# Retention samples in row and column groups, gated transposes moved into the chunk loop, on-chip memory reordered

## What is computed

```python
def retention_step(s, (qc, kc, vc)):          # per head, state s is 128 x 128
    att = einsum("bihd,bjhd->bhij", qc, kc) * decay
    o = einsum("bhij,bjhe->bihe", att, vc) + einsum("bihd,bhde->bihe", qc * q_dec, s)
    s = s * c_dec + einsum("bjhd,bjhe->bhde", kc * k_dec, vc)

def gla_step(s, (qc, kc, vc, gc)):            # per head, state s is 128 x 256
    o = einsum("bhij,bjhe->bihe", att, vc) + einsum("bihd,bhde->bihe", qc * exp(b), s)
    s = s * exp(b_last) + einsum("bjhd,bjhe->bhde", kc * exp(b_last - b), vc)
```

## Time and profile before

| | us |
|---|---|
| runs shown | 2237.97, 2239.32, 2248.58 |
| median | 2239.32 |
| profiled execution, its own time | 2247.53 |
| its span | 2245.7 |
| PE busy | 2123.9 (95%) |
| DVE, ACT, POOL busy | 997.2, 762.3, 197.0 |
| stretch of the retention samples on PE | 153.25 to 172.19 |
| gated steps of heads 2 and 3 on PE | 1367.29 to 1413.43 |
| first half of `out1` with the gated samples | 1414.76 to 1473.15 |

### The profile page before, as it was taken

How to read it: one execution, slowest core, us unless ns; L and a number is a source line. 1 busy time by engine, 2 the same in 40 slices (tenths; PEclk the granted TensorE clock), 3 DMA queues, 4 the chain that set the end, 5 groups by cost and what they waited for, 6 DMA issues and landing times.

```text
span 2245.7 us, 30502 instructions
## 1 busy us (share of the span) xinstructions
PE 2123.9 (95%) x12346; PEld 1865.4 (83%) x12346; DVE 997.2 (44%) x1671; ACT 762.3 (34%) x1314; POOL 197.0 (9%) x454
## 2 busy tenths in 40 slices
PE   7999869999889999999999999899979999999997
PEld 6889649898668999999988888679857899999996
DVE  5451463334434444444343457552542544444443
ACT  3311442234423432322323446233542433233232
POOL 2020111000110000000000124110010000000001
PEclk9999888999999999999999999999999999999999
DMA  6232313124552212222222121432373122222221
GB/s 195 68 120 90 130 56 94 57 85 141 209 189 75 76 57 76 76 85 75 76 88 60 55 75 43 147 140 94 141 282 115 58 75 76 76 85 76 75 76 51
DMA packets 111048, 219.94 MB, mean 98 GB/s; under 512 B 6994, under 2 KB 52350, under 8 KB 110844
## 3 DMA queue, kind: packets, MB, share of 16 engines
q1 hardware_dynamic: 89920, 143.80, 19.3%
q0 software_dynamic: 20416, 72.09, 9.0%
q10 hardware_dynamic: 576, 2.10, 0.2%
HBM read 201.03 MB, written 18.24 MB: 98 GB/s over the span
## 4 chain that ended last, share of the span: by engine, by line
PE 88%; DVE 5%; ACT 3%; DMA 3%; issue 1%; POOL 0%; SPq 0%; ACTq 0%; DVEq 0%; POOLq 0%
PE bank L738 14%; PE bank L740 14%; PE bank L739 14%; PE bank L800 7%; PE bank L802 7%; PE bank L798 7%; PE bank L797 5%; PE bank L801 4%; PE bank L799 4%; PE bank L1092 1%; PE bank L761 1%; PE bank L1003 1%; PE bank L1070 1%; PE bank L1119 1%; DMA vcX<-cache_mem_v 1%
## 5 line engine op out<-in xcount | busy, mean ns | idle before, releaser
L1869 DVE TENSOR_TENSOR w_lo<-raw,w_hi 128x1024 fp32r<-128x1024 f32 x265 | 319.7, 1222 | 604.3 <-ACT w_hi L1395 600.4
L1395 ACT ACTIVATE w_hi<-raw 128x1024 fp32r<-128x1024 f32 x265 | 274.2, 1052 | 327.1 <-PE bank L740 266.8
L738 PE MATMUL bank<-w_hi,hT_lo 128*128 128x512 f32 x720 | 290.5, 403 | 7.5 <-DVE Sb L2377 4.0
L800 PE MATMUL bank<-hT_lo,w_hi 128*128 128x384 f32 (+1 forms) x856 | 289.3, 338 | 0.0
L798 PE MATMUL bank<-hT_hi,w_lo 128*128 128x384 f32 (+1 forms) x856 | 289.3, 338 | 0.0
L802 PE MATMUL bank<-hT_hi,w_hi 128*128 128x384 f32 (+1 forms) x856 | 289.3, 338 | 0.0
L740 PE MATMUL bank<-w_hi,hT_hi 128*128 128x512 f32 x720 | 285.8, 397 | 0.0
L739 PE MATMUL bank<-w_lo,hT_hi 128*128 128x512 f32 x720 | 285.7, 397 | 0.0
L797 PE MATMUL bank<-hT_hi,w_lo 128*128 128x256 f32 (+1 forms) x856 | 239.6, 280 | 0.0
L799 PE MATMUL bank<-hT_lo,w_hi 128*128 128x256 f32 (+1 forms) x856 | 239.0, 279 | 0.0
L801 PE MATMUL bank<-hT_hi,w_hi 128*128 128x256 f32 (+1 forms) x856 | 239.0, 279 | 0.0
(11 more groups left out here) (362 smaller groups left out, 3160.6 us busy)
## 6 DMA issues: line engine op xcount, KB each, us to landing
raw<-w_ffn_gate SPq DMA_DIRECT2D x44, 512.0 KB, 4.0
raw<-w_ffn_up SPq DMA_DIRECT2D x44, 512.0 KB, 5.1
raw<-w_ffn_down SPq DMA_DIRECT2D x22, 1024.0 KB, 5.0
kcX<-cache_mem_k POOLq DMA_DIRECT2D x16, 1024.0 KB, 7.6
vcX<-cache_mem_v POOLq DMA_DIRECT2D x16, 1024.0 KB, 7.3
raw<-w_in_even SPq DMA_DIRECT2D x14, 1024.0 KB, 5.2
raw<-w_in_odd SPq DMA_DIRECT2D x12, 1024.0 KB, 5.1
raw<-w_cq SPq DMA_DIRECT2D x8, 1024.0 KB, 7.8
```

The costliest lines, as they stand in the source:

```text
L738: pe.matmul(out, wl, xh, start=first, stop=False)
L800: pe.matmul(ob, wh, hT_lo[:, k, HA:TOK], start=False, stop=False)
L1395: act.activation(w_hi[:, g % W_SLOTS, 0:n], raw[:, q % 2, UNIT * i:UNIT * i + n], ACT.Copy).then_inc(*hi_made.mark(c, u))
L1869: dve.tensor_tensor(w_lo[:, s, 0:n], raw[:, q % 2, UNIT * i:UNIT * i + n], flat(w_hi[:, s, 0:n]), ALU.subtract).then_inc(*lo_made.mark(c, u))
```

## The change

**Memory.** `w_hi`, `w_lo` and `hT` now come first, then the shared region `U`, then `raw`, `x` and the rest. The four retention states get other places: head 0 over `kd0`'s first tiles, heads 1 and 2 over `xn`, head 3 over `gain`. SP's load of the cross-attention gain waits for the store of the last retention state instead of the bias row. ACT waits for that store before the key projection's evacuation and no longer before the query projection's.

**Retention samples.** POOL issues the loads of heads 1 to 3 right after the first norm and the bias rows, that of head 0 after prompt tile 1, and clears the (smaller) `qz0` then. `ret_padded` makes all padding at once, before the last prompt tile's mask. PE reads in column groups: the query tile has 192 columns per head, and four sequences sit in four 32-column groups. It adds in row groups: two masks split even and odd sequences, four groups of 32 rows go to four banks. Reads of all heads come first, then the additions of heads 0 and 1, one column tile of the next projection, the additions of heads 2 and 3. DVE's state updates are sixteen of 256 columns instead of eight of 512.

**Gated transposes.** `MIXED_IN` puts the transposes of the first six half-tiles into the steps of heads 2 and 3, with ACT's copies and DVE's subtractions; the transposes of (1, 3), the split of unit 0 and the last state update move too.

```diff
-MIXED_FIRST = [(0, 0), (0, 1), (0, 2), (0, 3), (1, 0), (1, 1)]
+MIXED_IN = {(1, t): [(0, t)] + [(1, t - 2)] * (t >= 2) for t in range(TP)}
...
-        Sb0 = [at(f"Sb0{h}", off, [P, NB, P]) for h, off in enumerate((0, 20480, 4096, 24576))]
-        qz0 = at("qz0", 10240, [P, 2, 1152])
-        kz0 = [at("kz0a", 55296, [P, NB, P]), at("kz0b", 30720, [P, NB, P])]
+        Sb0 = [over(f"Sb0{h}", a, [P, NB, P]) for h, a in enumerate((U + 20480, xn_at, xn_at + 4096, gain_at))]
+        qz0 = at("qz0", 10240, [P, H, 192])
+        kz0 = at("kz0", 55296, [P, 2, 512])
...
+            pool.wait_ge(*aux_full.at("nT", "mix0", T - 1, 1))
+            for h in range(1, H):
+                ret_state(h)
             for t in range(TP - 1):
                 head_rstd(("ret", t), t, H, P)
                 if t == 1:
                     ret_state(0)
-                    ret_state(1)
-            pool.wait_ge(*aux_full.at("att0", TP))
-            pool.memset(qz0[:, :, :], 0.0).then_inc(*pool_done.mark("qz0"))
+                    pool.memset(qz0[:, :, :], 0.0).then_inc(*pool_done.mark("qz0"))
...
-                for b in range(NB):
-                    ins = pe.matmul(o[:, P * h:P * h + P], qz0[:, h % 2, P * b:P * b + P], Sb0[h][:, b, :], start=False, stop=b == NB - 1)
+                for c in range(2):
+                    for g in range(4):
+                        ins = pe.matmul(o[32 * g:32 * g + 32, e], qz0[:, h, 48 * g + 16 * c:48 * g + 16 * c + 32], Sb0[h][:, 2 * g + c, :],
+                                        start=False, stop=c == 1, tile_position=(0, 32 * g))
...
+            def add_pair(hp):
+                banks = [(aux if g < 2 else lin).open(pe, "s0s", hp, g) for g in range(4)]
...
             for i in range(4):
+                if i < 2:
+                    add_pair(i)
                 cols_tile(("in0", 0), "mix0", P * i, i, last=i == 3)
...
                     proj_tile(c, "mix1", tt)
+                for m in MIXED_IN.get((hp, t), ()):
+                    mixed_turn(*m)
                 pe.wait_ge(*dve_done.at("qe", hp, t))
...
-            for q, t in MIXED_FIRST:
-                mixed_turn(q, t)
+            mixed_turn(1, 2)
             out1(0)
-            mixed_turn(1, 2)
             out1(1)
             read_state(0)
             read_state(1)
+            mixed_turn(1, 3)
             add_state(0)
-            mixed_turn(1, 3)
             out1(2)
             read_state(2)
             read_state(3)
             add_state(1)
             out1(3)
-            add_state(2)
             for hp in range(2):
                 mixed_turn(hp, TP)
             pe_done.after("mixed", 1)
+            add_state(2)
+            out1(TP)
             add_state(3)
-            out1(TP)
```

More of the change, by code:

```diff
@@ L445, in gains @@
                 if nm == "cross0":
-                    sp.wait_ge(*put["bias"].at("row"))
+                    sp.wait_ge(*put["st0"].at(H - 1))
                 if nm == "cross1":
@@ new lines, in _ @@
+            ins.then_inc(*aux_full.mark("o0", TP))
+            def add_pair(hp):
+                banks = [(aux if g < 2 else lin).open(pe, "s0s", hp, g) for g in range(4)]
+                for hh in range(2):
+                    for c in range(2):
+                        for g in range(4):
+                            r = slice(32 * g, 32 * g + 32)
+                            e = slice(P * (2 * hp + hh), P * (2 * hp + hh) + P)
+                            ins = pe.matmul(banks[g][:, P * (2 * hh + c):P * (2 * hh + c) + P], kz0[r, c, e], bv[r, TP, e], start=True, stop=True, tile_position=(32 * g, 0))
+                            if hh and c:
+                                ins.then_inc(*(aux_full if g < 2 else lin_full).mark("s0s", hp, g))
@@ L1820, in _ @@
                     split_hi(NEXT[c], [0])
+                if t == TP - 1 and hp:
+                    gate_tile(1, TP)
+                for q, u in MIXED_IN.get((hp, t), ()):
+                    mixed_hi("mixC", u, q)
                 if t == TP - 1:
-                    if hp:
-                        gate_tile(1, TP)
                     split_hi(NEXT[c], [1, 2, 3])
@@ L2009, in ret_out, with ret_padded @@
                 dve_done.after("of", "ret", t)
[L2011 to L2016, removed]
-                dve.tensor_copy(qz0[:, h % 2, :].rearrange("p (b w) -> p b w", b=NB)[:, :, 0:TS], bqT[:, TP, h, :].rearrange("p (b q) -> p b q", b=NB)).then_inc(*dve_done.mark("qz0", h))
-                dve.tensor_tensor(kz0[h % 2][:, :, :], bcast(kd0[:, TP, P * h:P * h + P], 1, NB), bcast(seq_mask[:, :], 2, P), ALU.mult).then_inc(*dve_done.mark("kz0", h))
+            def ret_padded():
+                dve.wait_ge(*pool_done.at("qz0"))
+                q = bqT[:, TP, :, :].rearrange("p h (g c w) -> p (h g) c w", c=2, w=TS)
+                slots = qz0[:, :, :].rearrange("p h (g c w) -> p (h g) c w", c=3, w=TS)
+                for c in range(2):
+                    ins = dve.tensor_copy(slots[:, :, 2 * c, :], q[:, :, c, :])
+                ins.then_inc(*dve_done.mark("qz0"))
+                for c in range(2):
+                    ins = dve.tensor_scalar(kz0[:, c, :], kd0[:, TP, :], lam_mask[:, c:c + 1], None, ALU.mult)
+                ins.then_inc(*dve_done.mark("kz0"))
             for t in range(TP):
+                if t == TP - 1:
+                    ret_padded()
                 mask_att(t, att0)
@@ L2040, in _ @@
                     ret_tail(t)
-            dve.wait_ge(*pe_done.at("ret_p"))
-            ret_padded(1)
             ret_tail(TP - 1)
-            for h in range(H):
-                if 1 <= h < H - 1:
-                    ret_padded(h + 1)
-                for n in range(2):
-                    s = Sb0[h][:, 4 * n:4 * n + 4, :]
-                    dve.wait_ge(*lin_full.at("s0s", h, n))
-                    dve.scalar_tensor_tensor(s, s, gam[h] ** TS, lin.bank("s0s", h, n)[:, :].rearrange("p (b e) -> p b e", b=4), ALU.mult, ALU.add).then_inc(*lin_v.mark("s0s", h, n))
-                dve_done.after("S0new", h)
-            ret_out(TP)
+            dve.wait_ge(*dve_done.at("ret_out", TP - 1))
+            ret_out(TP)
+            for hp in range(2):
+                for g in range(4):
+                    full, banks, drained = (aux_full, aux, aux_v) if g < 2 else (lin_full, lin, lin_v)
+                    dve.wait_ge(*full.at("s0s", hp, g))
+                    for h in (2 * hp, 2 * hp + 1):
+                        s = Sb0[h][:, 2 * g:2 * g + 2, :]
+                        new = banks.bank("s0s", hp, g)[:, 256 * (h % 2):256 * (h % 2) + 256].rearrange("p (c e) -> p c e", c=2)
+                        ins = dve.scalar_tensor_tensor(s, s, gam[h] ** TS, new, ALU.mult, ALU.add)
+                    ins.then_inc(*drained.mark("s0s", hp, g))
+                dve_done.after("S0new", 2 * hp)
+                dve_done.after("S0new", 2 * hp + 1)
             ret_tail(TP)
@@ L2334, in _ @@
                     split_lo(NEXT[c], [0])
+                for q, u in MIXED_IN.get((hp, t), ()):
+                    mixed_lo("mixC", u, q)
                 if t == TP - 1:
```

52 lines of the change are left out of this document (19 added, 33 removed).

## The result

The changed kernel takes 2207.89 us (median of four runs, 2204.11 to 2210.56), the kernel before 2240.64 (2237.97 to 2248.58). The ratio is 0.9837, 95% interval 0.9816 to 0.9859: faster by 1.6%; the two medians lie 33 us (1.5%) apart.

What follows compares the result with a forecast made beforehand. PE, with 88% of the chain, was taken as the bound: its program plus waits and low clock. Gains of 8.8 (retention), 11.3 (gated) and 0 (memory) sum to 20.1 us: 2239.3 - 20.1 = 2219.2 us, range 2211 to 2231.

Steps and rivals of the forecast that it cites:

- Part 1, waits: Retention samples: PE's waits of 1.59 us (padding) and 1.77 us (head 2's state) go, 3.4 us, with nothing late instead.
- Part 1, pace: Retention samples: grouped records keep the measured 0.0625 and 0.0675 us; 18.9 us become 10.1, gain 8.8 with waits included.
- rival (a): Retention samples: grouped records of 128 columns run at half the assumed time, 4.1 us more gain, 2215 us; chance 0.08.
- the fourfold rule: Retention samples: 128 grouped records cost a quarter of 0.115 us each, 3.7 us, for a gain of 13.4 us.
- Part 2: Gated transposes and their order: 14.85 us of waits and clock dips removed, 3.5 of new waits, gain 11.3 us.
- Three new waits of about 1.2 us: Gated end: PE waits for bank drains at third product, third addition and second half's first product, together 3.5 us.
- The first step's wait: Gated loop, first step of heads 2 and 3: first transposes fill 0.45 us of PE's 1.1 us wait.
- rival (d): Gated loop starves: PE waits in every step at low clock, up to 35 us more, 2254 us; chance 0.05.
- the dips: Gated part: low clock behind the three larger old waits goes, worth 1.6, 1.7 and 1.4 us.
- Part 3: Memory order of the whole kernel: no time depends on an address, so it was costed at nothing.
- The warning that ended the prediction: Matmuls elsewhere: if their mean time changes, memory order matters and the forecast is wrong altogether; no size given.
- The range's lower end: Whole kernel: 2211 us, from 2219.2 less 4.1 (half the pace) and 3.7 (no new waits).

Runs made afterwards that it cites:

- m_shift: The kernel before with only the start of shared region `U` moved 384 bytes later; ratio 0.9961 to the kernel before.
- w_off: The changed kernel with everything but `w_hi` and `w_lo` moved up by 128 bytes; a single run of 2228.77 us.
- ht_off: The changed kernel with both parts of `hT` moved up by 128 bytes, all else in place; ratio 0.994 to the kernel before.
- g_only: The kernel before with the gated part of the change alone, memory order and retention samples as before; ratio 0.9967 to the kernel before.

## Why the prediction was right or wrong

**Part 1, waits: right.** Padding and states were in time, the 3.4 us of waits are gone, no dip follows, and the additions' second block waits for no bank.

**Part 1, pace: the term that was mis-sized.** The step that failed is "I take the unchanged pace, because it is measured and the half is not". It put 64 x 0.0625 + 64 x 0.0675 = 8.3 us for the grouped records; they take 4 x 0.58 + 1.11 + 1.10 = 4.5. The nearest rows streamed 256 columns; at 128 columns the pace is 36 and 35 ns instead of 62 and 68. That reads and additions agreed to 8% did not prove a rate of issue: both streamed the same number of columns. The full-width records and changes of form came to 1.6 us against 1.8. So the part gave 12.9 us, rival (a) to the digit (in part by luck, since 4.5 and 1.6 us stand where it had 4.2 and 1.8), and the fourfold rule of the Trainium skill's "TensorEngine Tiling (Array Packing)", section Theoretical Speedup, came nearer (13.4) than my sum. Another page of the Trainium skill, "TensorE: Matmul & The Clock Gate", section "Wait — 56ns, not 53.3ns?", gives about 62 ns per MATMUL as a floor with hardware decode off. No run here shows that setting; a grouped record starts every 35 ns and a matmul, two records, every 70, so the trace neither shows such a floor nor rules it out.

**Part 2: right, term by term.** 43 us between the products were forecast, 43.3 came. Three new waits of about 1.2 us were forecast; they are 1.33, 1.14 and 0.64, at the three places named: the third product, the third addition, the first product of the second half. The first step's wait fell from 1.1 to 0.6 (0.45 forecast). The loop shows DVE busy for 32.0 of 37 us, with a clock of 1.00, so rival (d) did not come. The stretch gained 12.3 us against 11.3: 10.8 - 3.6 = 7.2 of waits (the forecast's terms net 6.65) and 5.1 that went with the dips (4.7). The dip at the cross-attention, which no run ties to the change, takes 1.6 of it back in the profiled execution, 10.7 in all. That forecast and result lie so close is partly luck: against the execution of m_shift, with the same gated code as before, the stretch gained 9.1.

**Part 3: wrong.** The step is "The page shows no time that depends on an address ... I cost it at nothing". It is worth 10.3 us by the traces (8.5 + 1.8), and 0.39% (0.19 to 0.58) alone in m_shift, 4 to 13 us. The two key tiles of the earlier trace rows lie 24 KB apart, so they have the same remainder by 256 and could not show it. The trace of before did: the same form at the same clock had two paces. Here are row products with `hT`, 15 matmuls from the first to the last of these rows:

```profile
1406.77 0.39 PE L738 MATMUL bank<-w_hi,hT_lo 128*128 128x512 f32 x1
...
1410.16 0.39 PE L738 MATMUL bank<-w_hi,hT_lo 128*128 128x512 f32 x1
```

3.39 / 15 = 226 ns, against 233.3 ns for the products with `a_hi` and `a_lo`. I had asked only whether one pair of tiles differed, and had not compared these two groups. The warning that ended the prediction (the mean time of matmuls elsewhere) was the right sign, but it had neither a price nor a rival.

**The sum.** 2240.6 - 12.9 - 12.3 - 10.3 + 1.6 = 2206.7 us; measured 2207.9. The terms come from single executions and the base from a median, so an agreement to 1 us is closer than they warrant. Of the 13.8 us beyond the forecast's 20.1, 10.3 are part 3, 4.1 the pace of part 1 and -0.6 part 2 with that dip. The range's lower end took in no gain from the memory order, and so the result fell outside.

## What to carry to other kernels

Before a memory layout is called neutral, compare the pace of all matmuls of one form at the same clock; if two groups differ, look at the remainders by 256 of their operands' addresses. When a form is priced from a row that streams another number of columns, both paces belong to the forecast, and the order in which groups follow one another is part of the price. A change of some us is read in the trace, start against start, since single whole times of this kernel scatter by more.

## What was not expected of the hardware

- A product of 128 x 512 with the stationary operand in `U` or `hT` starts every 226.9 ns when its remainder by 256 bytes equals that of the moving one, and every 232.4 (w_off) to 233.3 ns (before) at a difference of 64 or 128 bytes.
- Column products of 256 and 384 columns have three paces by block (54.3, 55.6 and 56.8 us for 380), at the same clock; the first and the last levels appear only in w_off and ht_off. What chooses between them is open.
- Records of 128 columns in four row groups start every 35 ns; with two neighbouring matmuls in one row group every 38, with four every 86.
- Low clock falls differently in each execution, with the same work. Windows of PE (us, PE busy, clock, DMA share, GB/s) in a stretch that no part changes, before and then g_only:

```profile
360.00:370.00 10.00, 10.00 (x56) 0.67 0.41 112
...
390.00:400.00 10.00, 9.62 (x39) 0.61 0.01 2
```

```profile
360.00:370.00 10.00, 10.00 (x78) 1.00 0.40 122
...
390.00:400.00 10.00, 8.99 (x41) 0.50 0.00 0
```

From 300 to 415 us, PE in g_only falls 5 us behind for this reason; by 700 us it has made that up. By the ratios the parts alone add up to 1.2% (0.39 + 0.46 + 0.33), the whole change gives 1.6%; the intervals of about 0.2 on each leave it open whether more than this scatter lies between.
